# Moving the activation parts, the gated parts and the arena of a two-block transformer kernel to other SBUF offsets

## The chip, the cores and the metric

The kernel runs on one core of one Trainium2 chip. The metric is the device time of one execution in microseconds, as the median of several runs. All work is float32; there is one input set and one output, (1, 256, 1024).

## The reference, cut to what matters

256 tokens of width 1024 pass through a first block (an S5 scan and an mLSTM side by side, cross attention over 256 memory rows, a convolutional feed-forward layer) and a second block (an even layer with two kinds of attention, an odd layer with four kinds, each followed by a feed-forward layer). The change touches every late matrix product. The largest share of them stands in the three feed-forward layers, each of this form with D_FF = 2816:

```python
def _conv_ffn(h, w_up, conv_w, conv_b, w_down):
    u = _causal_dwconv(h @ w_up, conv_w, conv_b)
    a, b = jnp.split(u, 2, axis=-1)
    return (jax.nn.gelu(a) * b) @ w_down
```

## The kernel before

**Precision.** The late products (all after the first mixer) are made of float32 matrices split in two: a high part, rounded to TensorE's fp32r type by ScalarE (L1469), and a low part, the difference, made by VectorE (L1480). A product is three matmuls into one accumulation: high by high, high by low, low by high. The activations are split in the same way (L1583 and L1589 for the transposed activations, L1863 and L1909 for the gated ones).

**Units.** The weights come in units of 1 MB (128 partitions by 2048 floats). SyncE loads a unit into one of three `raw` slots; ScalarE and VectorE split it into one of two slots of `w_parts`, or, for a few units at the start and end of a layer, into one of four places laid over the arena (`parts4096` to `parts16384`, in the profile all called `parts`). TensorE goes through the units in an order written out by hand. A few units (odd layer) are used unsplit, straight from `raw`, as plain float32.

**The order in a feed-forward layer** (11 chunks i of 256 columns). `pe_first` (L1729) does the two up units of chunk 0, `pe_up` (L1763) the 20 others: 48 matmuls per unit, weight tile 128x128 stationary, 256 activation columns moving. `pe_down` (L1782, in `pe_down_bank`) does the down unit of a chunk: 24 matmuls, the gated tile 128x128 stationary, 512 weight columns moving. The steady turn is one down unit (24 matmuls) and two up units (96 matmuls). The down unit of the last chunk (i = 10) lies in the place `parts4096`. The gated parts of chunk i are in buffer i % 2.

**Other late products.** L1533 has the weights stationary and the activations moving (as L1763). L1535, L1729 and L2176 have the activations stationary and the weights moving (L2176 is the output projection; two of its weight chunks are in `parts`).

**Where things lie.** `late_memory` (L1265) allocates per partition, in this order: `raw` (3 slots of 8192 bytes), `w_parts` (4 parts of 8192 bytes), `pad_x`, `hT_parts` (16384 bytes), `gT_parts` (8192 bytes), `pad_arena`, `arena_late`. LINE is 16 floats, 64 bytes. All starts of operands within a tile are multiples of 512 bytes from the tile's own start in all products named above but one form of L1729 (184 columns, 48 matmuls), so the place of an operand modulo 512 bytes is that of its tile. Counted from `w_parts`, modulo 512, they are: `raw` 0, `w_parts` 0, `hT_parts` 64, `gT_parts` 64, `arena_late` and `parts` 128.

In this text the *distance* of a matmul is the place of its stationary operand less the place of its moving operand, modulo 512 bytes. Before, it is:

| Products | stationary, moving | distance |
|---|---|---|
| L1763, L1533 | `w_parts`, `hT_parts` | 448 |
| L2176, L1535, part of L1729 | `hT_parts`, `w_parts` | 64 |
| most of L1729, a quarter of L2176 | `hT_parts`, `parts` | 448 |
| L1782, chunks 0 to 9 | `gT_parts`, `w_parts` | 64 |
| L1782, chunk 10 | `gT_parts`, `parts` | 448 |

The early products (L478, L480, L616) have places of their own, which come from the numbers in `setup_memory` (L144 on) times 4 bytes, modulo 512: `w0` 192, `w1` 64, `w2` 448, `w3` 64, the activations `yS`, `yG`, `yM`, `M` 0. In the order of `early_units` this gives distance 192 for the unit on yS, 64 and 448 for the two on yG, 192 and 64 for the two on yM, and 64, 320, 448, 448 for the four on M. The trace calls all four weight places `early_w_parts`.

Of the kernel before, what the change touches and what calls it, by code (L numbers as in the profile page):

```python
# [6 lines left out]
F32 = mybir.dt.float32  # L7
F32R = mybir.dt.float32r
# [3 lines left out]
ALU = mybir.AluOpType  # L12
AX = mybir.AxisListType

P = 128
SEQ, D, NT, KD = 256, 1024, 2, 8
# [14 lines left out]
LINE = 16  # L31
# [47 lines left out]
def shaped(a, dims):  # L79
    if len(dims) == 1:  # L80
        return a
    names = "abcd"[:len(dims)]
    return a.rearrange(f"p ({' '.join(names)}) -> p {' '.join(names)}", **dict(zip(names[1:], dims[1:])))


class Kernel:
# [1178 lines left out]
    def late_memory(self):  # L1265


        self.early.close()
        self.raw = self.sb("raw", [P, RAW, SLOT])

        self.w2p = self.sb("w_parts", [P, 2, 2, SLOT], F32R)
        self.sb("pad_x", [P, LINE])
        self.hTr = self.sb("hT_parts", [P, 2, KD, SEQ], F32R)[:, :, :, :]
        self.gTr = self.sb("gT_parts", [P, 2, 2, 2, SEQ], F32R)
        self.sb("pad_arena", [P, LINE])
        self.arena_cols = 26624

        self.over = {}
        for at in (4096, 8192, 12288, 16384):
            with ExitStack() as c:  # L1280
                c.enter_context(self.nc.sbuf_tensor(f"below{at}", [P, at], F32))
                self.over[at] = c.enter_context(self.nc.sbuf_tensor(f"parts{at}", [P, 2, SLOT], F32R))
        self.ar = self.sb("arena_late", [P, self.arena_cols])
        self.hparts = (self.hTr[:, 0], self.hTr[:, 1])
        self.att_at, self.bt_at = 0, self.arena_cols - NCLS * 256
# [490 lines left out]

    def pe_down_bank(self, i, tt, hf, stop=False):
        wh, wl = (shaped(a, (2, D)) for a in self.parts_of(self.ff["d", i]))
        gh, gl = self.gTr[:, i % 2, 0], self.gTr[:, i % 2, 1]
        for m in range(2):  # L1780
            for q, (g, w) in enumerate(((gh, wh), (gh, wl), (gl, wh))):
                mm = self.T.matmul(self.ps[:, 2 * tt + hf, :], g[:, m, tt * P:(tt + 1) * P], w[:, m, hf * 512:(hf + 1) * 512],  # L1782
                                   start=False, stop=stop and m == 1 and q == 2, skip_group_check=True)
        return mm
# [72 lines left out]
    def act_high(self, i):  # L1857

        if self.ff_kind == 1:
            self.A.wait_ge(*self.s_prod.next("A"))  # L1860
        else:
            self.A.wait_ge(*self.drained(self.ff_fills["b", i]))
        self.done(self.A, self.A.copy(self.gTr[:, i % 2, 0], self.g32[i % 2]), self.s_ghi)  # L1863

    def dve_ffn(self, cols, out):
        self.dve_freed(out[WAY_OUT[1]])
# [31 lines left out]
    def dve_gate(self, i):  # L1898
        V, p = self.V, i % 2
        y, g, fb = self.y[p], self.g32[p], self.ff_fills["b", i]  # L1900
        V.wait_ge(*self.s_gelu.next("V"))
        if self.ff_kind == 1:
            self.done(V, V.tensor_tensor(g, y[0], y[1], ALU.mult), self.s_prod)
        else:
            V.wait_ge(*self.full(fb))
            ins = V.tensor_tensor(g, y[0], self.bank2(fb), ALU.mult)  # L1906
            self.drain(V, ins, fb)
        V.wait_ge(*self.s_ghi.next("V"))
        self.done(V, V.tensor_tensor(self.gTr[:, p, 1], g, self.gTr[:, p, 0].bitcast(F32), ALU.subtract), self.s_g)  # L1909

# [1187 lines left out]
```

## Time and profile before

| | |
|---|---|
| Median of 3 runs (lowest, highest) | 1266.45 us (1266.42, 1271.71) |
| The profiled execution's own time | 1264.75 us |
| Its span in the profile | 1263.4 us |
| TensorE matmuls, busy | 1221.4 us (97%) |
| VectorE, ScalarE, GpSimd busy | 901.2, 609.1, 107.8 us |
| DMA | 202.76 MB, mean 160 GB/s |

How to read it: the span is that of the instructions of the program; the execution's own time is 1.35 us longer. A matmul's record has a modelled end, so the length of one record (about 280 ns for 256 columns) is not its cost in a stream. What one costs is the spacing of the starts. In a merged timeline row of n matmuls this is the row's length less one record, divided by n - 1.

### The profile page before, as it was taken

The numbers are of one execution on the slowest core, as the hardware profiler recorded it, in microseconds if no ns is written. First come the engines' busy times: TensorE is split into PE (matmuls) and PEld (weight loads), VectorE is DVE, ScalarE is ACT, GpSimd is POOL, SyncE is SP. The second block draws the span as 40 slices with busy tenths as digits, with TensorE's granted clock in tenths as the row PEclk, the third lists the DMA queues.
The fourth block names the chain that finished last, engine by engine and source line by source line (L and its number), as shares of the span: only waits on it lengthen the run. The fifth ranks groups of instructions, "written<-read, shape, count | busy, mean of one in ns | idle before, by whom it ended". The sixth has DMA issues, their size and how long they took to land. (4 is left out here: it accounts for less than half of the span.)

```text
span 1263.4 us, 21186 instructions
## 1 busy us (share of the span) xinstructions
PE 1221.4 (97%) x8525; PEld 1120.7 (89%) x8528; DVE 901.2 (71%) x1266; ACT 609.1 (48%) x919; POOL 107.8 (9%) x148
## 2 busy tenths in 40 slices
PE   8999999989999999999998999999999999999997
PEld 5888888979999999899988999998987898999996
DVE  5977996675767888845778666767665589666677
ACT  2252123453755666634664555554423464645552
POOL 3893000003000000010000000000200000000000
PEclk9999999999999999999999999999999799999999
DMA  9553444526726667625334456667455105555560
GB/s 278 175 153 108 133 134 143 194 88 195 244 89 200 211 223 228 206 69 160 109 101 167 157 177 229 198 231 167 101 163 185 33 1 174 193 177 191 191 208 35
DMA packets 178734, 202.76 MB, mean 160 GB/s; under 512 B 21884, under 2 KB 163163, under 8 KB 178636
## 3 DMA queue, kind: packets, MB, share of 16 engines
q1 hardware_dynamic: 175083, 191.49, 47.6%
q0 software_dynamic: 3184, 9.77, 2.6%
q8 instruction: 68, 1.11, 0.4%
q10 hardware_dynamic: 369, 0.13, 0.1%
q14 instruction: 30, 0.25, 0.1%
HBM read 200.30 MB, written 1.08 MB: 159 GB/s over the span
## 5 line engine op out<-in xcount | busy, mean ns | idle before, releaser
L1480 DVE TENSOR_TENSOR w_parts<-raw,w_parts 128x1024 fp32r<-128x1024 f32 (+1 forms) x242 | 294.9, 1219 | 131.7 <-ACT w_parts L1469 126.3
L1763 PEld LDWEIGHTS ps<-hT_parts,w_parts 128*128 128x128 f32 x2880 | 342.8, 188 | 2.3
L1763 PE MATMUL ps<-hT_parts,w_parts 128*128 128x256 f32 x2880 | 344.5, 280 | 0.0
L1469 ACT CAST w_parts<-raw 128x1024 fp32r<-128x1024 f32 (+1 forms) x242 | 253.1, 1046 | 166.2 <-PE ps L1763 64.5
L1782 PE MATMUL ps<-w_parts,gT_parts 128*128 128x512 f32 x720 | 173.5, 395 | 1.1 <-DVE w_parts L1480 1.1
L1782 PEld LDWEIGHTS ps<-w_parts,gT_parts 128*128 128x128 f32 x720 | 133.1, 187 | 32.4 <-DVE w_parts L1480 1.3
L478 PE MATMUL ps<-hT,ring 128*128 128x256 f32 x448 | 100.3, 384 | 1.2 <-DVE hT L321 1.2
L1533 PE MATMUL ps<-hT_parts,w_parts 128*128 128x256 f32 x816 | 99.3, 281 | 2.2 <-DVE w_parts L1480 1.6
L1533 PEld LDWEIGHTS ps<-hT_parts,w_parts 128*128 128x128 f32 x816 | 97.0, 188 | 2.9 <-DVE w_parts L1480 1.8
L478 PEld LDWEIGHTS ps<-hT,ring 128*128 128x128 f32 x448 | 85.7, 193 | 14.4 <-issue 1.6
L1887 DVE SCALAR_TENSOR_TENSOR arena_late<-ps,vecT,arena_late 128x255 f32<-128x255 f32 (+1 forms) x176 | 84.9, 482 | 10.5 <-ACT arena_late L1837 4.2
L1729 PE MATMUL ps<-parts,hT_parts 128*128 128x256 f32 (+1 forms) x576 | 72.6, 282 | 4.5 <-DVE hT_parts L1589 4.1
L1729 PEld LDWEIGHTS ps<-parts,hT_parts 128*128 128x128 f32 x576 | 68.4, 188 | 6.9 <-issue 3.8
L1863 ACT CAST gT_parts<-arena_late 128x512 fp32r<-128x512 f32 x33 | 20.5, 621 | 79.6 <-DVE arena_late L1906 43.9
L1837 ACT ACTIVATE arena_late<-ps,vecT 128x256 f32<-128x256 f32 x88 | 49.7, 565 | 4.9 <-PE ps L1747 2.0
L2176 PE MATMUL ps<-w_parts,hT_parts 128*128 128x256 f32 x396 | 49.0, 280 | 1.2 <-DVE w_parts L1480 1.2
L2176 PEld LDWEIGHTS ps<-w_parts,hT_parts 128*128 128x128 f32 x396 | 46.6, 188 | 1.8 <-DVE w_parts L1480 1.8
L1589 DVE TENSOR_TENSOR hT_parts<-ps,hT_parts 128x512 fp32r<-128x512 f32 (+1 forms) x36 | 24.4, 677 | 33.1 <-ACT hT_parts L1583 32.6
L1583 ACT CAST hT_parts<-ps 128x512 fp32r<-128x512 f32 (+1 forms) x36 | 20.7, 574 | 55.9 <-PE ps L1564 55.7
L2010 ACT ACTIVATE arena_late<-arena_late,small 128x128 f32<-128x128 f32 (+3 forms) x72 | 35.3, 491 | 22.6 <-DVE small L2053 20.7
L1480 DVE TENSOR_TENSOR parts<-raw,parts 128x1024 fp32r<-128x1024 f32 (+2 forms) x36 | 43.0, 1193 | 2.6 <-ACT parts L1469 1.6
L1909 DVE TENSOR_TENSOR gT_parts<-arena_late,gT_parts 128x512 fp32r<-128x512 f32 x33 | 22.9, 693 | 28.9 <-ACT gT_parts L1863 28.9
(413 smaller groups left out, 1564.4 us busy)
## 6 DMA issues: line engine op xcount, KB each, us to landing
raw<-in_ffn_w_up SPq DMA_DIRECT2D x44, 1024.0 KB, 5.1
raw<-in_f_w_up SPq DMA_DIRECT2D x22, 1024.0 KB, 5.2
raw<-in_ffn_w_down SPq DMA_DIRECT2D x22, 1024.0 KB, 5.0
ring<-in_w_in SPq DMA_DIRECT2D x18, 1024.0 KB, 5.8
raw<-in_ev_w_in SPq DMA_DIRECT2D x15, 1024.0 KB, 5.4
raw<-in_f_w_down SPq DMA_DIRECT2D x11, 1024.0 KB, 4.9
ring<-in_x_wkv SPq DMA_DIRECT2D x8, 1024.0 KB, 5.6
ring<-in_w_out SPq DMA_DIRECT2D x4, 1024.0 KB, 8.1
```

What stands on the lines that cost most here:

```text
L478: mm = T.matmul(o, w[:, kk, hh * 256 + j * P:hh * 256 + (j + 1) * P], x[:, kk, :], start=first, stop=last)
L1469: self.done(A, A.copy(high[:, c], self.raw[:, u % RAW, c]), self.s_hi)
L1480: self.done(V, V.tensor_tensor(low[:, c], self.raw[:, u % RAW, c], high[:, c].bitcast(F32), ALU.subtract), self.s_lo)
L1533: mm = T.matmul(o, w[:, kk, hh * 256 + j * P:hh * 256 + (j + 1) * P], x[:, kk, :], start=first, stop=last)
L1589: self.drain(V, V.tensor_tensor(self.tile_part(1, i, n), self.tile_bank(f, n), self.tile_part(0, i, n).bitcast(F32), ALU.subtract), f)
L1729: mm = T.matmul(self.ps[:, b, t * n[j]:(t + 1) * n[j]], x[:, kk, t * P:(t + 1) * P], w[:, kk, :], start=kk == 0 and q == 0, stop=kk == KD ...
L1763: mm = T.matmul(self.ps[:, b, m * 256:m * 256 + 256], w[:, kk, m * P:(m + 1) * P], x[:, kk, :], start=kk == 0 and q == 0, stop=kk == KD - ...
L1782: mm = self.T.matmul(self.ps[:, 2 * tt + hf, :], g[:, m, tt * P:(tt + 1) * P], w[:, m, hf * 512:(hf + 1) * 512], start=False, stop=stop an ...
L1837: ins = A.activation(y[:, m, :], bank[:, m, :], ACT.Identity, bias=cols("b", n, 2 * i + m), scale=cols(2, n, 2 * i + m))
L1887: ins = V.scalar_tensor_tensor(y[:, m, d:SEQ], bank[:, m, 0:SEQ - d], cols(tap, n, 2 * i + m), y[:, m, d:SEQ], ALU.mult, ALU.add)
L2010: ins = A.activation(self.sc[p][:, c0:c0 + w], src[:, c0:c0 + w], ACT.Exp, bias=self.nm[b][:, j:j + 1], scale=scale, accum_out=self.dn[b][ ...
L2176: mm = T.matmul(o, x[:, kk, tt * P:(tt + 1) * P], w[:, kk, :], start=kk == 0 and q == 0, stop=kk == k - 1 and q == 2)
```

## The change

It alters sizes of padding and splits the gated buffer in two allocations. `pad_x` grows from 64 to 256 bytes; the two gated buffers get pads of 448 and 192 bytes before them; `pad_arena` grows from 64 to 128 bytes; the arena is 256 floats shorter, and with it the bias tables at its upper end (`bt_at`) start 256 floats lower. No instruction is added or removed.

```diff
         self.w2p = self.sb("w_parts", [P, 2, 2, SLOT], F32R)
-        self.sb("pad_x", [P, LINE])
+        self.sb("pad_x", [P, 4 * LINE])
         self.hTr = self.sb("hT_parts", [P, 2, KD, SEQ], F32R)[:, :, :, :]
-        self.gTr = self.sb("gT_parts", [P, 2, 2, 2, SEQ], F32R)
-        self.sb("pad_arena", [P, LINE])
-        self.arena_cols = 26624
+        self.gTr = []
+        for i, pad in enumerate((7, 3)):
+            self.sb(f"pad_g{i}", [P, pad * LINE])
+            self.gTr.append(self.sb(f"g{i}T_parts", [P, 2, 2, SEQ], F32R))
+        self.sb("pad_arena", [P, 2 * LINE])
+        self.arena_cols = 26624 - 256
@@ pe_down_bank
-        gh, gl = self.gTr[:, i % 2, 0], self.gTr[:, i % 2, 1]
+        gh, gl = self.gTr[i % 2][:, 0], self.gTr[i % 2][:, 1]
@@ act_high
-        self.done(self.A, self.A.copy(self.gTr[:, i % 2, 0], self.g32[i % 2]), self.s_ghi)
+        self.done(self.A, self.A.copy(self.gTr[i % 2][:, 0], self.g32[i % 2]), self.s_ghi)
@@ dve_gate
-        self.done(V, V.tensor_tensor(self.gTr[:, p, 1], g, self.gTr[:, p, 0].bitcast(F32), ALU.subtract), self.s_g)
+        self.done(V, V.tensor_tensor(self.gTr[p][:, 1], g, self.gTr[p][:, 0].bitcast(F32), ALU.subtract), self.s_g)
```

Counted from `w_parts` modulo 512, the places become: `hT_parts` 256, the gated buffer of even chunks 256 + 448 = 192, that of odd chunks 192 + 192 = 384 (each buffer is 4096 bytes), `arena_late` and `parts` 384 + 128 = 0. The distances become:

| Products | distance before | distance after |
|---|---|---|
| L1763, L1533 | 448 | 256 |
| L2176, L1535, part of L1729 | 64 | 256 |
| most of L1729, a quarter of L2176 | 448 | 256 |
| L1782, even chunks 0 to 8 | 64 | 192 |
| L1782, odd chunks | 64 | 384 |
| L1782, chunk 10 | 448 | 192 |

## Rows read from the trace of the kernel before

**Rows 1.** The page, busy time of the engines: busy us (share of the span) and instructions.
```profile
PE 1221.4 (97%) x8525; PEld 1120.7 (89%) x8528; DVE 901.2 (71%) x1266; ACT 609.1 (48%) x919; POOL 107.8 (9%) x148
```

**Rows 2.** The page, span in 40 slices: the granted TensorE clock.
```profile
PEclk9999999999999999999999999999999799999999
```

**Rows 3.** Waits of PE, the longest: us in total, times, longest.
```profile
PE ps L1729 <- DVE hT_parts L1589: 4.3, 6, 1.3
```

**Rows 4.** The chain that ended last, third feed-forward layer: start, us, what.
```profile
1108.51 5.60 PE ps L1782 x24
1114.11 11.30 PE ps L1763 x96
...
1215.55 22.61 PE ps L1763 x192
```

**Rows 5.** Windows: PE, PEld, DVE, ACT, POOL busy (instructions), clock, DMA share, GB/s.
```profile
385.00:401.90 16.90, 16.90 (x123) 15.79 (x121) 12.57 (x17) 9.81 (x12) 0.00 (x0) 1.00 0.57 189
...
545.00:733.00 188.00, 179.98 (x1458) 173.83 (x1457) 128.49 (x185) 98.53 (x167) 7.37 (x9) 1.00 0.42 134
```

**Rows 6.** Lines by form, PE: count | busy us, mean ns of one record | idle before.
```profile
L1763 PE MATMUL ps<-hT_parts,w_parts 128*128 128x256 f32 x2880 | 344.5, 280 | 0.0
L1782 PE MATMUL ps<-w_parts,gT_parts 128*128 128x512 f32 x720 | 173.5, 395 | 1.1 <-DVE w_parts L1480 1.1
...
L1533 PE MATMUL ps<-hT_parts,w_parts 128*128 128x256 f32 x816 | 99.3, 281 | 2.2 <-DVE w_parts L1480 1.6 <-DVE arena_late L2921 0.6
L1729 PE MATMUL ps<-parts,hT_parts 128*128 128x256 f32 x528 | 67.1, 282 | 4.5 <-DVE hT_parts L1589 4.1
L2176 PE MATMUL ps<-w_parts,hT_parts 128*128 128x256 f32 x396 | 49.0, 280 | 1.2 <-DVE w_parts L1480 1.2
...
L1535 PE MATMUL ps<-w_parts,hT_parts 128*128 128x256 f32 x144 | 17.7, 281 | 0.0
...
L2176 PE MATMUL ps<-parts,hT_parts 128*128 128x256 f32 x132 | 16.7, 281 | 1.3 <-DVE X L2189 1.3
```

**Rows 7.** Timeline of PE after a short wait, weights stationary: start, us, what, count.
```profile
861.03 5.49 PE L1763 MATMUL ps<-hT_parts,w_parts 128*128 128x256 f32 x47
...
916.79 5.38 PE L1533 MATMUL ps<-hT_parts,w_parts 128*128 128x256 f32 x46
```

**Rows 8.** Timeline of PE, late products with the activations stationary.
```profile
338.00 2.99 PE L2176 MATMUL ps<-parts,hT_parts 128*128 128x256 f32 x24
340.83 5.61 PE L2176 MATMUL ps<-w_parts,hT_parts 128*128 128x256 f32 x48
...
363.33 3.00 PE L1729 MATMUL ps<-parts,hT_parts 128*128 128x256 f32 x25
...
618.09 3.82 PE L1535 MATMUL ps<-w_parts,hT_parts 128*128 128x256 f32 x31
...
1075.55 2.99 PE L1729 MATMUL ps<-parts,hT_parts 128*128 128x256 f32 x24
```

**Rows 9.** Timeline of PE, early products at distances 192, 320 and 448, in this order.
```profile
242.23 5.34 PE L478 MATMUL ps<-early_yM_parts,early_w_parts 128*128 128x256 f32 x44
...
261.91 2.77 PE L616 MATMUL ps<-early_w_parts,early_M_parts 128*128 128x256 f32 x23
...
264.52 5.81 PE L616 MATMUL ps<-early_w_parts,early_M_parts 128*128 128x256 f32 x48
```

**Rows 10.** Timeline of PE, down units at the end of a feed-forward layer.
```profile
1238.00 8.56 PE L1782 MATMUL ps<-w_parts,gT_parts 128*128 128x512 f32 x36
1246.40 2.92 PE L1782 MATMUL ps<-parts,gT_parts 128*128 128x512 f32 x12
1249.15 2.96 PE L1782 MATMUL ps<-w_parts,gT_parts 128*128 128x512 f32 x12
```

**Rows 11.** Timeline of PE, plain float32 products; then the chain, 64-column products.
```profile
957.20 7.07 PE L1535 MATMUL ps<-raw,arena_late 128*128 128x256 f32 x32
...
1034.64 1.73 PE ps L1964 x16
```

## The prediction

> **What bounds the kernel now.** I read the page first, for which engine is full. TensorE's matmuls are busy 97% of the span, VectorE 71%, ScalarE 48% [rows 1], and TensorE's clock stands at its upper level (2.4 GHz) in all but one slice [rows 2]. Then PE's waits: the longest in total is 4.3 us [rows 3]. So the kernel is a queue of matmuls, and its length is count times spacing. In the chain that ended last the third feed-forward layer is nothing but matmuls in blocks: 24 down matmuls in 5.60 us, 96 up matmuls in 11.30, 192 in 22.61 [rows 4]: 233.3 ns and 117.8 ns each. The 256 columns of an up matmul at 2.4 GHz would take 106.7, so each spends 11 ns on something else, and the only thing that this change can touch is that.
>
> **The spacing has two levels.** The same line on the same tiles, at the same clock, runs at another spacing elsewhere. The 47 L1763 matmuls from 861.03 take (5490 - 280) / 46 = 113.3 ns, the 46 of L1533 from 916.79 (5380 - 280) / 45 = 113.3 [rows 7], both after a short wait of TensorE, both at distance 448, where otherwise 117.8 rules [rows 4]. Nothing between is found: a run sits at 113.3 or at 117.8. So the two streams that TensorE reads, the moving operand and the weights of the next matmul, lock into a rhythm, and there are at least two.
>
> Which rhythm is taken does hang on the distance. L2176 goes from distance 448 to 64 and back without a wait: the starts 338.00, 340.83 and the record rule give 2830 / 24 = 117.9 at 448, then (5610 - 280) / 47 = 113.4 at 64 [rows 8]. The early products, entered without a pause: 192 runs at (5340 - 280) / 43 = 117.7, 320 at (2770 - 280) / 22 = 113.2, and right behind it 448 at (5810 - 280) / 47 = 117.7 [rows 9]. But a run that begins after a wait keeps the rhythm it fell into: L1535 at distance 64 runs at (3820 - 280) / 30 = 118.0, and L1729 at distance 448 once at (3000 - 280) / 24 = 113.3 and once at (2990 - 280) / 23 = 117.8 [rows 8]. In sum: 64 and 320 draw to the fast level, 192 and 448 to the slow one, and a wait can override it.
>
> Distance 256, which the change gives to every up matmul and every projection, has no row. It lies between 192 (slow) and 320 (fast). If the pattern repeats every 256 bytes, as the pairs 64/320 and 192/448 suggest, 256 is the same as 0. That distance occurs only where two kinds of matmul meet: the last up matmul runs beside the load of a gated tile, both at place 64, and the last down matmul beside the load of a weight tile, both at 0. These meetings cost nothing to be seen: a block of 96 with one such meeting takes 11.30 us, half of 22.61, which has one in 192 [rows 4]. That speaks against 0 being much worse than 448, and no more.
>
> **The change part by part.** It adds and removes no instruction, DMA or wait; only addresses change.
>
> *Up matmuls, L1763, distance 448 to 256.* Bounds: below, the weight load alone sets the pace, which the 64-column products show at 1730 / 16 = 108 ns [rows 11]; above, one more step of the size between the two levels, 117.8 + 4.5 = 122.3. I take 113.3, the level that this line already reaches [rows 7], since the present value is the worse of the two known. 2880 - 48 now at 113.3 = 2832, times 4.5 ns = 12.7 us.
>
> *L1533, 816 matmuls [rows 6], the same distances.* 768 x 4.5 = 3.5 us. They stand in the attention stretches, where TensorE is idle 8 us of 188 [rows 5] for chains through softmax; I take half, 1.7.
>
> *L1729, 528 matmuls from `parts`, 448 to 256.* They are now at either level [rows 8]; half of them gain: 264 x 4.5 = 1.2 us.
>
> *L2176: 132 from `parts` (448 to 256)* gain 0.6 us. *Its 396 others and L1535's 144 (64 to 256)* are mostly fast now and I leave them there: 0, with a loss of up to 540 x 4.5 = 2.4 if 256 is slow.
>
> *Down matmuls, L1782.* At distance 64: 8400 / 36 = 233.3 ns; chunk 10 at distance 448: 2750 / 12 = 229.2 [rows 10]. For 512 columns the order of the two distances is thus the reverse of that for 256. Even chunks go to 192, which behaves as 448 where both are seen [rows 4, 9]: 5 chunks x 24 x 3 layers = 360 matmuls gain 4.1 ns, 1.5 us. Odd chunks go to 384, which has no row: I take 0, with bounds 216 ns (the plain float32 products stream at (7070 - 380) / 31 = 215.8 [rows 11]) and 237.4, a step of 4.1 up: -6.2 to +1.5 us for 360.
>
> *Two separate buffers, the shorter arena, lower bias tables:* VectorE and ScalarE read and write the same shapes. They are costed at nothing, hidden by TensorE: in the fullest turn VectorE is busy 12.57 of 16.90 us, ScalarE 9.81, the DMA engines 0.57 [rows 5]. With turns of 96 x 113.3 + 24 x 231 = 16.4 us the cover still holds, so a faster TensorE is not caught by its suppliers; were it, the next thing late would be the split of the next unit.
>
> The sum is 12.7 + 1.7 + 1.2 + 0.6 + 1.5 = 17.7 us. From the profiled execution's 1264.75 that gives 1247.0; the median is 1.7 us above that execution, so I predict 1266.45 - 17.7 = 1248.7.
>
> **A rule that speaks against it.** The trace has one line at 113.3 and 117.8 ns with nothing waiting [rows 4, 7]. The Trainium skill, page "SBUF — State Buffer", section "Who interferes with whom", gives TensorE two independent read ports, one for the moving operand and one for weight loads, and says that TensorE never waits on anyone. By that rule no offset matters and the sum is 0; this trace does not agree as far as two rhythms follow the distance [rows 8, 9].
>
> **Rivals.**
>
> *No effect.* The rhythm is chosen by the moment at which a run begins, and 256 is entered as 448 is. For it: L1535 slow at 64, L1729 fast at 448 [rows 8]. Against it: the immediate changes in L2176 and the early units [rows 8, 9]. Only the even down chunks might move: 1265 to 1266.
>
> *Slower.* Distance 256 is a third, slower rhythm. If the two streams start in the same place of a 256-byte pattern they could meet most often. The price at 122.3: L1763 12.7 + 0.4, L1533 1.7, L1729 264 x 4.5 + 264 x 9 = 3.6, L2176 and L1535 0.6 + 540 x 9 = 5.5, down 1.5, together 25.4: 1291.9. It decides once the mean spacing of these 4500 matmuls is above 117.8 + 6.3 / 4.5 = 119.2. Against it: the unpriced meetings at 0 [rows 4]. A mild form, in which 256 is like 448 and only the fast ones are lost, costs 2.4 + 1.2 + 0.3 = 3.9 us: 1270.4.
>
> *Full speed.* At 256 the streams never meet: 108 and 216 ns. L1763 2832 x 9.8 = 27.8, L1533 3.8, L1729 528 x 7.5 = 4.0, L2176 and L1535 132 x 9.8 + 540 x 5.3 = 4.2, down 792 x 17.3 = 13.7: 53.5, 1213. Against it: no long fp32r run of 256 columns goes under 113.
>
> **How the numbers follow.** My forecast 0.42, its own range 1244 to 1254; full speed or half-way to it 0.09; no effect 0.15; the mild loss 0.10; slower 0.24. A change under 0.5% (6.3 us) can't be told from none. Faster by more: 0.42 + 0.09 = 0.51; within: 0.15 + 0.10 = 0.25; slower: 0.24. The range leaves out most of full speed and the upper end of the slower case: 1236 to 1287.
>
> **What will show it.** In the chain of the changed kernel, 96 L1763 matmuls in 10.88 us instead of 11.30 show the step that carries the sum; 11.30 the rival without effect; 11.74 the slower one. 24 L1782 matmuls take 5.50 on even chunks and show 384's price on odd ones. L2176 on `w_parts` stays at 113.4 or shows the mild loss. Durations of the splits, the DMA's landing and PE's waits stay as they are; if PE's waits grow by more than 2 us, the cover was thinner than I read it. The prediction is wrong if 256 is not fast, which is the one value here taken without a row.

## The result and the profile after

The changed kernel takes 1277.05 us, the median of 6 runs (1276.04 to 1280.44), against 1267.54 for the kernel before (6 runs, 1266.42 to 1271.71). The ratio on record is 1.0082, with an interval of 1.0064 to 1.0100; the quotient of the two medians is 1.0075. So it is slower by 0.8%, some 9.5 us, where I had forecast 17.7 us less. (One run of a later kernel, with down at 192, took 2027.04 us at a mean granted clock of 0.55 and is left out of that kernel's median and ratio.) The profiled execution is one of 1276.81 us with a span of 1275.5. The page shows a TensorE as full as before [rows 1], with the clock at its upper level in all slices but two [rows 2]:

```profile
PE 1234.6 (97%) x8528; PEld 1134.9 (89%) x8528; DVE 900.7 (71%) x1266; ACT 609.0 (48%) x919; POOL 107.9 (8%) x148
...
PEclk8999999999999999999999999999999899999999
```

TensorE's matmuls grew by 13.2 us, the work of the other engines not at all. Line numbers have moved: L1763 of the kernel before is L1766 here, and L1767 in the kernels of the experiments that leave out a pad of size 0. The chain that ended last, third feed-forward layer (start, us, what), answers to [rows 4]:

```profile
1102.39 5.50 PE ps L1785 x24
1107.89 11.52 PE ps L1766 x96
1119.41 5.59 PE ps L1785 x24
...
1227.31 23.03 PE ps L1766 x192
```

Each row's time divided by its count is the time of one matmul. An up matmul takes 23.03 / 192 = 119.9 ns instead of 117.8; I write 120.0, the commonest spacing of single starts. A down matmul takes 5.50 / 24 = 229.2 on even chunks (distance 192) and 5.59 / 24 = 232.9 on odd ones (384), instead of 233.3. The lines by form answer to [rows 6]:

```profile
L1766 PE MATMUL ps<-hT_parts,w_parts 128*128 128x256 f32 x2880 | 350.7, 283 | 0.0
L1536 PE MATMUL ps<-hT_parts,w_parts 128*128 128x256 f32 x816 | 101.3, 285 | 2.0 <-DVE w_parts L1483 1.4 <-DVE arena_late L2924 0.6
L1785 PE MATMUL ps<-w_parts,g1T_parts 128*128 128x512 f32 x360 | 86.7, 395 | 0.0
L1785 PE MATMUL ps<-w_parts,g0T_parts 128*128 128x512 f32 x360 | 85.6, 394 | 0.8 <-DVE w_parts L1483 0.8
L1732 PE MATMUL ps<-parts,hT_parts 128*128 128x256 f32 x528 | 68.7, 286 | 4.3 <-DVE hT_parts L1592 3.8
L2179 PE MATMUL ps<-w_parts,hT_parts 128*128 128x256 f32 x396 | 51.0, 285 | 0.8 <-DVE w_parts L1483 0.7
```

Every form with 256 columns whose distance changed has grown: 6.2, 2.0, 1.6 and 2.0 us for the four lines here. Of the lines whose distance changed only the down matmuls have shrunk, by 1.2. That the loss is no matter of feed-forward layers alone is seen in the output projection, timeline of TensorE after the change:

```profile
342.90 3.04 PE L2179 MATMUL ps<-parts,hT_parts 128*128 128x256 f32 x24
345.78 5.92 PE L2179 MATMUL ps<-w_parts,hT_parts 128*128 128x256 f32 x48
```

By the record rule these take (3040 - 280) / 23 = 120.0 and (5920 - 280) / 47 = 120.0 ns. The same two products ran at 117.9 and 113.4 [rows 8]; distance 256 has made them equal.

The 12.1 us between the two spans are not all the change's. The late section, in which all moved tiles are used, starts at 277.25 us before and at about 281.5 after. The windows of this section, before and then after (us, PE, PEld, DVE, ACT, POOL busy, clock, DMA share, GB/s):

```profile
277.25:1263.40 986.15, 952.21 (x6957) 886.82 (x6958) 687.82 (x947) 516.25 (x775) 28.15 (x44) 0.99 0.50 161
```

```profile
281.50:1275.50 994.00, 963.02 (x6961) 898.86 (x6959) 687.99 (x947) 515.67 (x773) 28.15 (x44) 0.99 0.50 159
```

So the section is longer by 7.8 us: 10.8 more of matmuls and 3.0 less of idle TensorE (33.9 to 31.0). That fits a slower TensorE that finds its suppliers ready more often. The other 4 us lie ahead of it, where no tile has moved. One part of them is a load that came later, 4.8 us of waiting in the first row of the waits after, against 3.0 in the trace before, and another the clock, granted at 0.98 on average in this stretch after and at 0.99 before:

```profile
PE ps L533 <- DMA small<-in_s_log_dt: 4.8, 1, 4.8
PE ps L1732 <- DVE hT_parts L1592: 3.8, 4, 1.3
```

The later waits (the second row answers to [rows 3]) have not grown. That the 4 us belong to this one execution is seen in a second profile of the changed kernel (the last pair of the experiments, span 1273.3 us). There the transposes with which the late section begins start at 278.33 us, 1.1 us later than before, and the section is 8.8 us longer than before:

```profile
278.33 0.60 PE L1567 MATMUL ps<-cst,arena_late 128*128 128x128 f32 x4
```

### The profile page after: what moved, and what is told of

The parts are those of the page before. It is cut to its first block and busy times, and to the rows that moved or that the text cites. A ratio compares the mean times of both kernels' runs of the same rounds, so it can differ in the third digit from the quotient of the medians.

```text
span 1275.5 us, 21189 instructions
## 1 busy us (share of the span) xinstructions
PE 1234.6 (97%) x8528; PEld 1134.9 (89%) x8528; DVE 900.7 (71%) x1266; ACT 609.0 (48%) x919; POOL 107.9 (8%) x148
## 5 line engine op out<-in xcount | busy, mean ns | idle before, releaser
L1766 PEld LDWEIGHTS ps<-hT_parts,w_parts 128*128 128x128 f32 x2880 | 349.1, 190 | 2.1
L1766 PE MATMUL ps<-hT_parts,w_parts 128*128 128x256 f32 x2880 | 350.7, 283 | 0.0
L1536 PE MATMUL ps<-hT_parts,w_parts 128*128 128x256 f32 x816 | 101.3, 285 | 2.0 <-DVE w_parts L1483 1.4
L1536 PEld LDWEIGHTS ps<-hT_parts,w_parts 128*128 128x128 f32 x816 | 99.0, 192 | 2.7 <-DVE w_parts L1483 1.7
L1785 PE MATMUL ps<-w_parts,g1T_parts 128*128 128x512 f32 x360 | 86.7, 395 | 0.0
L1785 PE MATMUL ps<-w_parts,g0T_parts 128*128 128x512 f32 x360 | 85.6, 394 | 0.8 <-DVE w_parts L1483 0.8
L1785 PEld LDWEIGHTS ps<-w_parts,g1T_parts 128*128 128x128 f32 x360 | 66.8, 188 | 15.1
L1785 PEld LDWEIGHTS ps<-w_parts,g0T_parts 128*128 128x128 f32 x360 | 66.8, 188 | 15.1 <-DVE w_parts L1483 1.0
L2179 PE MATMUL ps<-w_parts,hT_parts 128*128 128x256 f32 x396 | 51.0, 285 | 0.8 <-DVE w_parts L1483 0.7
L2179 PEld LDWEIGHTS ps<-w_parts,hT_parts 128*128 128x128 f32 x396 | 48.5, 192 | 1.3 <-DVE w_parts L1483 1.2
```

Source lines behind the costliest of these rows:

```text
L1536: mm = T.matmul(o, w[:, kk, hh * 256 + j * P:hh * 256 + (j + 1) * P], x[:, kk, :], start=first, stop=last)
L1766: mm = T.matmul(self.ps[:, b, m * 256:m * 256 + 256], w[:, kk, m * P:(m + 1) * P], x[:, kk, :], start=kk == 0 and q == 0, stop=kk == KD - ...
L2179: mm = T.matmul(o, x[:, kk, tt * P:(tt + 1) * P], w[:, kk, :], start=kk == 0 and q == 0, stop=kk == k - 1 and q == 2)
```

## The experiments

**Which of the moved tiles costs the time.** The first kernel takes the changed one and puts the gated buffers back to 64 from the weights. Up stays at distance 256, down returns to 64, and the arena is kept at 0.

```diff
-        for i, pad in enumerate((7, 3)):
-            self.sb(f"pad_g{i}", [P, pad * LINE])
+        for i, pad in enumerate((5, 0)):
+            if pad:
+                self.sb(f"pad_g{i}", [P, pad * LINE])
...
-        self.sb("pad_arena", [P, 2 * LINE])
+        self.sb("pad_arena", [P, 7 * LINE])
```

> The activations' place alone as in the change: hT_parts at 256 and the arena at 0, so every up matmul and projection has distance 256; the gated parts stay at 64, so the down matmuls of chunks 0 to 9 keep distance 64. Distance theory: the up matmuls run at 120.0 ns as in the changed kernel, the down matmuls at 233.3 as before, and the kernel is 11 to 13 us slower than before (2832 x 2.2 ns + 816 x 2.2 + about 1000 that were at 113.3 x 6.7). Rival, the gated buffers or their separation cost the time: within 3 us of before.

1277.53 us (4 runs, 1274.77 to 1279.37) against 1267.24 (13 runs); ratio 1.0077, interval 1.0050 to 1.0104. Its chain:

```profile
1101.36 5.60 PE ps L1786 x24
1106.96 11.51 PE ps L1767 x96
```

Down is back at 233.3 ns, up stands at 119.9. So the loss of up (10.3 us by the medians, where I expected 11 to 13) needs no move of the gated buffers. The arena's place is not separated here; the pair at the end does that.

The second kernel does the other half alone: `hT_parts` stays at 64 and the arena at 128, the gated buffers go to 192 and 384.

```diff
-        self.sb("pad_x", [P, 4 * LINE])
+        self.sb("pad_x", [P, 1 * LINE])
...
-        for i, pad in enumerate((7, 3)):
+        for i, pad in enumerate((2, 3)):
...
-        self.sb("pad_arena", [P, 2 * LINE])
+        self.sb("pad_arena", [P, 4 * LINE])
```

> The gated buffers alone as in the change: 192 and 384 from the weights, hT_parts still at 64 and the arena at 128. Distance theory: even down units at 229.1 ns, odd ones at 232.6, up matmuls at 117.8, and the kernel is 1.5 to 2 us faster than before. Rival, the gated buffers or their separation cost the time: 8 us slower.

1265.49 us (10 runs, 1262.72 to 1269.13); ratio 0.9983, interval 0.9969 to 0.9997. Its chain:

```profile
1092.16 5.50 PE ps L1785 x24
1097.65 11.31 PE ps L1766 x96
```

Down on even chunks takes 229.2 ns as in the changed kernel, up 117.8 as before. The gated part is a gain of some 2 us by the medians; the interval reaches from 0.4 to 3.9.

**Spacing against distance, alone.** A probe that does none of the reference's work: it copies x to the output and issues blocks of 48 float32r matmuls of 256 columns. One block stands for each distance from 0 to 480 in steps of 32 bytes, first each after a wait, then without a wait up and down the list. The last blocks have both operands 32 bytes higher. No other engine touches the memory during a block; between the blocks that wait, VectorE writes one column of a small tile.

```python
for k in range(48):
    s = 256 * (k % 8) + shift // 4
    m = 512 * (k % 4) + shift // 4
    f(ps[:, b, 0:256], s, m, ...)
def d064(o, s, m, a, z):   # d000: m + 0, d032: m + 120, d096: m + 104, ...
    T.matmul(o, st[:, s:s + 128], mv[:, m + 112:m + 112 + 256], start=a, stop=z)
```

> A probe instead of the kernel: it does none of the reference's work but copies x to the output. It runs blocks of 48 fp32r matmuls of 256 columns, a weight tile of 128 columns each, at 16 distances of 32 bytes, nothing else running; first each block after a wait, then blocks following each other without a wait, then with both operands moved by 32 bytes. Distance theory: the spacing is a function of the distance alone; 113.3 at 64 and 320, 117.8 at 192 and 448, 120.0 at 256, with a period of 256 bytes 0 would be 120.0 also. Rival, the operands' own place counts and not their distance: moving both by 32 bytes changes the spacings. Rival, traffic of the other engines makes the levels: here all are equal, near 108.

Timeline of TensorE in the probe. The lines stand for distances: L47 0, L50 32, L53 64, L56 96, L59 128, L62 160, L65 192, L68 224, L71 256, L77 320.

```profile
24.53 5.92 PE L53 MATMUL ps<-moving,stationary 128*128 128x256 f32 x48 [0.18 <-DVE small L130]
...
150.21 11.52 PE L50 MATMUL ps<-moving,stationary 128*128 128x256 f32 x96
161.56 5.79 PE L56 MATMUL ps<-moving,stationary 128*128 128x256 f32 x48
167.19 5.92 PE L62 MATMUL ps<-moving,stationary 128*128 128x256 f32 x48
172.95 5.76 PE L68 MATMUL ps<-moving,stationary 128*128 128x256 f32 x48
...
212.63 5.82 PE L77 MATMUL ps<-moving,stationary 128*128 128x256 f32 x48
218.28 5.91 PE L71 MATMUL ps<-moving,stationary 128*128 128x256 f32 x48
...
235.38 5.63 PE L53 MATMUL ps<-moving,stationary 128*128 128x256 f32 x48
240.86 11.66 PE L47 MATMUL ps<-moving,stationary 128*128 128x256 f32 x96
...
257.82 5.86 PE L59 MATMUL ps<-moving,stationary 128*128 128x256 f32 x48
263.52 5.81 PE L65 MATMUL ps<-moving,stationary 128*128 128x256 f32 x48
...
274.93 5.62 PE L77 MATMUL ps<-moving,stationary 128*128 128x256 f32 x48
...
298.28 5.72 PE L53 MATMUL ps<-moving,stationary 128*128 128x256 f32 x48 [0.18 <-DVE small L130]
```

By the record rule, in ns:

| distance modulo 256 | 0 | 32 | 64 | 96 | 128 | 160 | 192 | 224 |
|---|---|---|---|---|---|---|---|---|
| 256 columns | 119.8 | 118.3 | 113.6 or 117.9 | 117.2 or 118.7 | 118.7 | 120.0 | 117.7 | 116.6 |

Three things are read here. Distances 0 and 256 (L47, L71) are the same, and so are the other pairs but for the two places with two levels, 64 and 96: the period is 256 bytes. Distance 256 costs 120 ns with nothing else running, at a granted clock of 1.00, so no other engine is needed for it. Distance 64 (and 320) has two levels by how it is entered. L77 runs at (5820 - 280) / 47 = 117.9 behind a block at distance 384 and at 113.6 behind one at 256. A row that begins after a wait is some 0.10 us longer for the start. Less that, the L53 at 24.53 runs at (5820 - 280) / 47 = 117.9, the slow level, and the one at 298.28, with both operands 32 bytes higher, at 113.6, the fast one. So my rival, that the operands' own place counts, came true at distance 64 (and 320). At 128, 192, 256, 384 and 448 the same shift changed no row by more than 0.02 us.

**The same with 512 columns.** The probe with N = 512 and 24 matmuls in a block.

> The same probe with 512 columns and 24 matmuls per block; it too does nothing of the reference's work. Distance theory: 233.3 ns at 64, 229.1 at 192 and 448, 232.6 at 384; a period of 256 bytes makes 128 the same as 384. Rival, traffic of the other engines makes the levels: all near 216.

```profile
236.25 11.06 PE L47 MATMUL ps<-moving,stationary 128*128 128x512 f32 x48
247.15 5.76 PE L53 MATMUL ps<-moving,stationary 128*128 128x512 f32 x24
252.75 5.73 PE L59 MATMUL ps<-moving,stationary 128*128 128x512 f32 x24
258.32 5.66 PE L65 MATMUL ps<-moving,stationary 128*128 128x512 f32 x24
```

With 0.39 us for a record: (11060 - 390) / 47 = 227.0 ns at distance 0, 233.5 at 64, 232.2 at 128, 229.1 at 192. These are the levels of the down matmuls: 233.3 at 64, 229.2 at 192, 232.9 at 384, which is 128. The best distance for 512 columns is 0, one of the two worst for 256.

**Two layouts from the map.** If down is best at 0 and up at 320, both may be had: the gated buffers at 256, `hT_parts` at 192. The first kernel takes both steps (arena at 384), the second only moves the gated buffers of the kernel before to 256 and leaves `hT_parts` at 64.

```diff
-        self.sb("pad_x", [P, 4 * LINE])
+        self.sb("pad_x", [P, 3 * LINE])      # second kernel: 1 * LINE
...
-        for i, pad in enumerate((7, 3)):
+        for i, pad in enumerate((1, 0)):     # second kernel: (3, 0)
...
         self.sb("pad_arena", [P, 2 * LINE])  # second kernel: 6 * LINE
-        self.arena_cols = 26624 - 256
+        self.arena_cols = 26624              # second kernel: 26624 - 256
```

> Places chosen from the probe's map: hT_parts at 192, both gated buffers at 256, the arena at 384. Up matmuls (L1763, L1533) get distance 320, which is 64 modulo 256, projections on w_parts 192, those on parts 320, down matmuls 256, which is 0 modulo 256. Distance theory with the map: down matmuls at 226.7 ns (720 x 6.6 = 4.8 us less than before), up matmuls at 113.3 if each run locks into the faster rhythm (2832 x 4.5 = 12.7 and about 2 on L1533, 2 on parts, less 2 lost on L2176 and L1535): 18 to 20 us faster than before. If the rhythm entered after a down unit is the slower one, up matmuls stay at 117.8 and the kernel is 3 to 7 us faster. Rival, the probe's map does not hold beside the other engines' traffic: no change.

> The gated part alone, at the place that the map shows best: both gated buffers at 256, hT_parts and the arena as before. Distance theory: down matmuls of chunks 0 to 9 at 226.7 instead of 233.3 ns (4.8 us), chunk 10 at 232.4 instead of 229.2 (0.2 us lost), up matmuls unchanged at 117.8: 4 to 5 us faster than before. Rival, the down units have slack behind the splits: less than 2 us.

They take 1264.37 us (12 runs, 1261.12 to 1267.86; ratio 0.9978, interval 0.9965 to 0.9990) and 1263.93 us (12 runs, 1258.74 to 1271.01; ratio 0.9980, interval 0.9963 to 0.9997), against 1267.09. Chain of the first:

```profile
1107.35 5.44 PE ps L1786 x24
1112.79 11.31 PE ps L1767 x96
```

Down reaches 226.7 ns as the probe says. Up, at distance 320, stays at 117.8 in this chain: the fast rhythm was allowed and not taken. So of the 18 to 20 us of my expectation only the part of the down matmuls came. That gain itself is also smaller than the 720 x 6.6 ns = 4.8 us of its sum: in busy time the 720 down matmuls fell by 4.0 and 3.3 us, and 0.2% is 2.5 to 2.8 us, though the intervals reach to 4.4 and 4.7. My 4 to 5 us for the second kernel missed too.

**Does the down block hand over a rhythm?** A probe with the kernel's own turns (no work of the reference): 24 down matmuls, 96 up matmuls at distance 64, three turns in a row. The gated tile is at 0, 64, 128 and 192 bytes, then all of it again 32 bytes higher.

> A probe; it does none of the reference's work but copies x to the output. It runs the feed-forward layer's steady turn, 24 down matmuls and then 96 up matmuls, three times over, with up at distance 64 and down at 0, 64, 128 and 192, first at the late tiles' own places, then all moved by 32 bytes. Which of the two rhythms, 113.3 or 117.8 ns, the up block takes: if the down block's rhythm hands it over, it is the same in each turn and depends on the down distance (at 0 the slow one, as in v3's kernel); if it is chance, turns at the same distance differ.

Timeline of TensorE, up blocks only; L54 stands behind down at 0, L60 behind 64, L66 behind 128, L72 behind 192.

```profile
36.07 11.47 PE L54 MATMUL ps<-moving,stationary 128*128 128x256 f32 x96
...
70.18 11.06 PE L60 MATMUL ps<-moving,stationary 128*128 128x256 f32 x96
...
86.67 11.47 PE L60 MATMUL ps<-moving,stationary 128*128 128x256 f32 x96
...
137.38 11.05 PE L66 MATMUL ps<-moving,stationary 128*128 128x256 f32 x96
...
187.09 11.07 PE L72 MATMUL ps<-moving,stationary 128*128 128x256 f32 x96
```

11.47 is (11470 - 280) / 95 = 117.8 ns and 11.06 is 113.5. Behind down at 0 every up block is slow. Behind 64 the blocks alternate: fast, slow, fast. Behind 128 the first is slow and the others fast. Behind 192 all are fast, and all slow once everything is moved by 32 bytes. The level of an up block at 64 is thus settled in the probe by what ran ahead of it and by the absolute place, and in a way that repeats; the alternation shows that more is carried over than the distance of the last down block.

**The layout that this points to.** Up at 320, down at 192 on all chunks:

```diff
-        self.sb("pad_x", [P, 4 * LINE])
+        self.sb("pad_x", [P, 3 * LINE])
...
-        for i, pad in enumerate((7, 3)):
+        for i, pad in enumerate((0, 0)):
...
-        self.sb("pad_arena", [P, 2 * LINE])
-        self.arena_cols = 26624 - 256
+        self.sb("pad_arena", [P, 3 * LINE])
+        self.arena_cols = 26624
```

> As v3, but with both gated buffers at 192, so the down matmuls of chunks 0 to 9 have distance 192. By the map they run at 229 instead of 226.7 ns (1.7 us more than v3). If a down block at 192 hands over the fast rhythm, the up matmuls fall to 113.3 and the kernel is 15 us faster than before; if not, it is within 3 us of before.

1255.19 us is the median of five runs (1254.26 to 1261.02), against 1267.77 (11 runs); ratio 0.9918, interval 0.9891 to 0.9944. Its chain in the third feed-forward layer, then a row of the timeline and one of the waits of L1767 (us in total, times):

```profile
1108.26 10.91 PE ps L1767 x96
1119.17 5.49 PE ps L1786 x24
```

```profile
469.83 11.47 PE L1767 MATMUL ps<-hT_parts,w_parts 128*128 128x256 f32 x96
```

```profile
  DVE w_parts L1484: 1.6, 6
```

Up now takes 10.91 / 96 = 113.6 ns in the third layer. In the first layer it falls back to 117.8 for a time, as at 469.83, so the line's busy time falls from 344.5 us [rows 6] to 335.1, and not by the 12.7 that 113.3 throughout would give. The single starts show where this begins. The block at 452.96 runs at 113.3 for its first unit of 48; the next two gaps are 236 and 226 ns, a wait for VectorE's split of the second unit, and from there on it runs at 117.8. The next block, at 469.83, is slow from its first matmul, behind a down block at 192 that in the probe (without the shift) always led to the fast level. So a short wait inside a block can change the rhythm as well, and the down block does not always bring it back. The same view of the kernel before and of the changed kernel lists no wait for this line; the one pause of the kernel before that [rows 7] shows, ahead of 861.03, also changed the rhythm, there to the faster one.

**64 bytes off the change.** The changed kernel with `hT_parts` 64 bytes lower, which makes up 320 instead of 256 and leaves the gated buffers at 192 and 384 and the arena at 0; the arena gets its 256 floats back. Beside it stands the changed kernel itself on the same chip.

```diff
-        self.sb("pad_x", [P, 4 * LINE])
+        self.sb("pad_x", [P, 3 * LINE])
...
-        for i, pad in enumerate((7, 3)):
+        for i, pad in enumerate((0, 3)):
...
-        self.arena_cols = 26624 - 256
+        self.arena_cols = 26624
```

> The changed kernel with one thing altered: hT_parts lies 64 bytes lower, at 192 instead of 256; gated buffers (192, 384) and arena (0) stay where the change put them modulo 512, so up matmuls have distance 320 instead of 256. Theory of distance and entry: both down distances, 192 and 384 (128 modulo 256), hand the fast rhythm over in the probe of turns, so L1766's matmuls run near 114 instead of 120.0 ns, and the kernel is 16 to 20 us faster than the changed one and 7 to 11 us faster than before. Rival, the down distance of 384 breaks it: half of the up blocks at 117.8, 10 to 12 us faster than the changed one.

> The changed kernel itself once more, on the chip of the run beside it: 9 to 11 us slower than before, L1766 at 120.0 ns.

1256.74 us (5 runs, 1254.28 to 1257.87; ratio 0.9923, interval 0.9908 to 0.9937) and 1275.34 us (4 runs, 1274.04 to 1277.17; ratio 1.0075, interval 1.0061 to 1.0089), against 1266.16. Their chains, first the one with 64 bytes less:

```profile
1104.90 5.58 PE ps L1786 x24
1110.48 10.89 PE ps L1767 x96
```

```profile
1117.19 5.59 PE ps L1785 x24
1122.78 11.52 PE ps L1766 x96
```

The same instructions, the same down distances, the same arena place modulo 512; 64 bytes less before `hT_parts` are worth 18.6 us. So it is the place of `hT_parts`, and not that of the arena, that turns a gain into a loss.

**What does the level hang on?** A last probe (no work of the reference) at distances 0, 64, 128 and 192, with weight tiles of 128, 96, 64 and 32 columns, and with bf16 operands.

> A probe; it does none of the reference's work but copies x to the output. Blocks of 32 matmuls at distances 0, 64, 128 and 192 with weight tiles of 128, 96, 64 and 32 columns, 256 and 512 moving columns, in fp32r, then in bfloat16. If the time above streaming comes from the two reads meeting, it shrinks with the width of the weight tile (half of it at 64 columns) and depends less on the distance; in bfloat16, where both streams carry half the bytes, all distances stand near 108 and 216. If the moving stream alone costs it, the spacing does not depend on the width: 120 at distance 0 and 256 columns for every width.

Timeline: L50 and L53 are 256 float32r columns at distances 0 and 64 with the full weight tile, L86 and L89 the same with 32 weight columns; L146 and L164 are bf16 with 256 and 512 columns.

```profile
13.57 4.10 PE L50 MATMUL ps<-moving,stationary 128*128 128x256 f32 x32 [1.22 <-ACT moving_bf L184]
...
63.76 3.96 PE L86 MATMUL ps<-moving,stationary 128*32 128x256 f32 x32 [0.18 <-DVE small L196]
67.90 3.83 PE L89 MATMUL ps<-moving,stationary 128*32 128x256 f32 x32 [0.18 <-DVE small L196]
...
204.84 3.67 PE L146 MATMUL ps<-moving_bf,stationary_bf 128*128 128x256 bf16 x32 [0.19 <-DVE small L196]
...
234.79 7.08 PE L164 MATMUL ps<-moving_bf,stationary_bf 128*128 128x512 bf16 x32 [0.19 <-DVE small L196]
```

By single starts, without the start of each row, the full tile runs at 120.0, 117.8, 118.8 and 117.8 ns at distances 0, 64, 128 and 192, and the tile of 32 columns at 117.8, 113.3, 113.3 and 116.6. So a quarter of the columns leaves an excess over bf16 of 4 to 9 ns; it does not fall to a quarter. But the width does change which distance has which level: with 64 columns distance 0, the worst for the full tile, runs at 113.4. With 512 moving columns the full tile takes 227.8 to 233.4 ns by distance and the one of 32 columns 231.0 to 231.7: the distance hardly matters there, the excess stays. My expectation, that the excess shrinks with the width, fell for the most part, and that it depends less on the distance held at 512 columns. The map of the first probe is thus one for full tiles. Each form ran only once, after a wait. In bf16 there are no levels: 3.67 us at all four distances, 109.2 ns between single starts, and 7.08 us, 215.8 ns, for 512 columns. The probe changed the type of both operands at once, and so leaves open which of the two matters.

## Why the prediction was wrong

**What bounds the kernel** was right. It is a queue of matmuls at spacing times count, before and after, and no other engine's time has moved. The lines of 256 columns whose distance changed, some 5,000 matmuls, grew by 13.3 us in busy time, 2.7 ns on each.

**The step that failed** is "*Up matmuls, L1763, distance 448 to 256*", in its sentence "I take 113.3, the level that this line already reaches [rows 7], since the present value is the worse of the two known." The runs showed 120.0 in its place. With it fell the terms of L1533, L1729 and L2176, which used the same value: taken as -12.7, -1.7, -1.2 and -0.6 us, measured in busy time as +6.2, +2.0, +1.6 and +0.3. [rows 7] shows the line at 113.3 at distance 448, in runs after a wait. It says what the line can reach, and nothing on where distance 256 lies.

**Two sentences led there.** "Nothing between is found: a run sits at 113.3 or at 117.8" was true of the distances that the kernel before has, which are 64, 192, 320 and 448. Modulo 256 these are only 64 and 192. The probe has six other classes, of which five are at 117 or above and two of these at 120. That the period is 256 bytes I had guessed, and the guess held; it made 256 the same as 0, and so a class without any run. Then I let the meetings at 0 speak "against 0 being much worse than 448". One meeting in 96 matmuls shows at most its own few ns. A level is a property of a run.

**The slower rival** had the mechanism, distance 256 as a third, slower rhythm, and the point from which it decides, 119.2. Only its price was off: 122.3 against 120.0, one step of the known size against half of one. With 2.2 ns for the slow ones and 6.7 for the fast ones its sum is 6.6 + 2.0 + 2.3 + 3.9 - 1.5 = 13.3 us. Measured term by term in busy time they are 6.2, 2.0, 1.6, 2.8 and -1.2, together 11.4; all matmuls of the late section grew by 10.8. The section also had 3.0 us less of idle TensorE, which I had not counted, and is 7.8 us longer; in the second profile of the changed kernel it is 8.8. The rest of the 9.5 between the medians lies ahead of it. The rival's picture, two streams that start in the same place meet most often, is not borne out: with 512 columns distance 0 is the best, and with 256 distance 160 is as slow as 0. That the loss needs no move of the gated buffers is shown by the first experiment (1.0077), and that 64 bytes before `hT_parts` turn it round by the pair at the end (0.9923 and 1.0075).

**"I leave them there"** (L2176 and L1535 on `w_parts`, 64 to 256): this held a loss of up to 2.4 us as a bound. Measured, L2179 went from 49.0 to 51.0 us by its line and is at 120.0 where it was at 113.4, and L1538 (before L1535) from 17.7 to 18.2. The term put at nothing cost 2.5 us. The 96 matmuls of L1729 on `w_parts`, at distance 64 before as well, had no term and went from 13.3 to 14.0.

**The down matmuls** were right: -1.5 us forecast, -1.2 in busy time. Even chunks stand at 229.2, as read from chunk 10. Odd ones at 384 take 232.9 where I took 233.3, far within the bounds of 216 and 237.4. Alone, this part is worth 0.17%.

**The cover** was not tried by the changed kernel, in which TensorE was no faster; elsewhere it held, but only just. In the two kernels where it was, with turns of 16.4 us as I had worked out, the time fell by 0.8%, but the up line waited for VectorE's split 6 and 7 times, 1.6 and 1.8 us in all, where the same view of the kernel before lists no wait. That is the "next thing late" that the prediction named, and part of its price is that the rhythm changed behind some of these waits.

**Two bounds** were read from rows of another kind. The 108 ns of the 64-column products is a mean: single starts of that block are 111 to 112 ns apart, but for the first, which is 59. And the 215.8 of [rows 11], my floor for 512 columns of float32r, belongs to plain float32 products of 256 columns. The bf16 blocks of the last probe, 109.2 and 215.8 ns, are the nearer rows. Neither bound enters the sum.

**The rule that spoke against it.** This change moves only addresses, and the time moved by 0.8% up, and by 0.8% down with 64 bytes less. The Trainium skill, page "SBUF — State Buffer", section "Who interferes with whom", has TensorE's two read ports independent. For float32r the runs do not agree, in so far as the spacing follows the distance between the two operands; for bf16, with one spacing at all four distances tried, they do. On the floor, the Trainium skill, page "TensorE: Matmul & The Clock Gate", section "Back-to-back issue gap", puts an isolated matmul of N columns at the upper clock at N / 2.4 + 2.5 ns, an estimate of 109.2 for 256 columns and 215.8 for 512. The bf16 streams agree to 0.1 ns. The plain float32 stream of [rows 11] does not: it has 256 columns and takes 215.8. The float32r streams lie 4 to 11 ns above the first figure and 11 to 18 above the second.

**What was near.** 1277.05 lies within the range, since the range reached to the slower case. The forecast of the sign gave 0.51 to the wrong side. A class of distance without a row deserved no likeliest level.

## What to carry to other kernels

Where TensorE is the bound and runs float32r, the place of the stationary operand less that of the moving one, modulo 256 bytes, is a setting that costs nothing to change and moved this kernel by 1.5% between its ends: measure all eight classes in a probe without the kernel's work before choosing pads. Choose it for each column count and width of the weight tile by itself, and then run the layout, since the level of one block can be settled by the block ahead of it or by a short wait inside it: the best place for the down matmuls cost more than it gave. When a value has no row in the trace, a neighbour's best level is no estimate; give its bounds, and let the chances be as wide as they are.

## What the runs showed of the hardware

- Float32r matmuls, each with its own load of a full 128x128 weight tile, have levels by distance modulo 256 bytes at the upper clock: 113.3 to 120.0 ns with 256 columns and about 226.7 to 234 with 512. Their order differs between the two column counts (0 is among the slowest in the one and the fastest in the other).
- At distance 64 (256 columns) two rhythms are stable, 113.3 and 117.8 ns. What ran before the block plays a part, and so does the absolute place: after a wait, 32 bytes more on both operands changed 117.8 into 113.3, and behind down at 192 they changed 113.5 into 117.8. The handover repeated in every turn of the probe, also its alternation behind down at 64. In the kernel a wait of some 0.2 us inside a block changed 113.3 into 117.8.
- In bf16, with the full tile, all four distances give 109.2 ns (256 columns) and 215.8 (512).
- A weight tile of a quarter of the columns keeps an excess (113.3 to 117.8 ns with 256 columns, 231.0 to 231.7 with 512), but the distances change their order: 0 goes from 120.0 to 117.8 and 128 from 118.8 to 113.3.
- No engine but TensorE is needed for the levels and the handover, as the probes show. What in the memory or in TensorE's reads makes it stays open: nothing here tells a conflict of addresses from a conflict of timing, distances that are no multiple of 32 bytes were not tried, nor was one operand in bf16 with the other in float32r.
